# A hybrid S5, DeltaNet and expert layer on one core: decay rows by transposes, and a new deal of the z projections in the DeltaNet groups

## What is computed

```python
def chunked_gated_delta_rule(q, k, v, g, beta):
    ...
    g = jnp.cumsum(g, axis=-1)
    decay = jnp.exp(jnp.where(incl, g[..., :, None] - g[..., None, :], -jnp.inf))
    kb = k * beta[..., None]
    a_mat = jnp.where(strict, jnp.einsum('bhncd,bhnsd->bhncs', kb, k) * decay, 0.0)
    lower = a_mat + jnp.eye(C, dtype=a_mat.dtype)
    rhs = jnp.concatenate([v * beta[..., None], kb * jnp.exp(g)[..., None]], axis=-1)
    sol = lax.linalg.triangular_solve(lower, rhs, left_side=True, lower=True, unit_diagonal=True)
    ...
    attn_intra = jnp.where(incl, jnp.einsum('bhncd,bhnsd->bhncs', q, k) * decay, 0.0)
    ...

def deltanet_branch(qkv, z, beta_logit, decay_logit, conv_w, a_log, dt_bias, norm_w, w_dn_out):
    ...
    o = chunked_gated_delta_rule(q, k, v, g, beta)
    o = o * lax.rsqrt(jnp.mean(jnp.square(o), axis=-1, keepdims=True) + RMS_EPS)
    o = o * norm_w.astype(f32) * jax.nn.silu(z.astype(f32).reshape(bsz, T, DN_V_HEADS, DN_HEAD_DIM))
```

## Time and profile before

| | |
|---|---|
| median of 3 runs | 2986.1 us |
| the profiled execution | 2986.08 us, span 2984.3 us |
| busy: PE, PE's weight loads | 2900.1 us (97%), 2086.5 us (70%) |
| busy: DVE, ACT, POOL | 912.0, 517.6, 100.5 us |
| mean granted TensorE clock | 0.992 |
| DeltaNet groups | about 67 to 983 us |
| S5 and the outputs | to about 1990 us |
| experts | from there to the end |

### The profile page before, as it was taken

The page is one execution under the profiler, slowest core; times in us unless marked ns, Lnnn a source line. Parts: engine busy times, 40 slices in busy tenths (PEclk is TensorE's granted clock), DMA queues, the critical chain, the costliest instruction groups (busy, mean ns, idle before and its releaser), DMA issues.

```text
span 2984.3 us, 47457 instructions
## 1 busy us (share of the span) xinstructions
PE 2900.1 (97%) x19639; PEld 2086.5 (70%) x19639; DVE 912.0 (31%) x2066; ACT 517.6 (17%) x809; POOL 100.5 (3%) x179
## 2 busy tenths in 40 slices
PE   8999999999999999999999999999999999999996
PEld 7888788888888888888888888873444444444442
DVE  1433424424334307777730000130121112111214
ACT  2221222222212132111010000121111111112110
POOL 2010011000100000000000000000000000000000
PEclk9999999999999999999999999999999999999998
DMA  6243342332434524244347665258899999999996
GB/s 195 81 131 99 98 125 91 101 123 80 138 94 113 154 95 136 92 127 128 122 145 218 197 194 171 112 204 361 362 422 422 422 422 422 422 422 422 422 422 261
DMA packets 325775, 654.05 MB, mean 219 GB/s; under 512 B 45232, under 2 KB 274736, under 8 KB 275440
## 3 DMA queue, kind: packets, MB, share of 16 engines
q1 hardware_dynamic: 325616, 651.61, 59.4%
HBM read 649.49 MB, written 2.10 MB: 218 GB/s over the span
## 4 chain that ended last, share of the span: by engine, by line
PE 58%; issue 16%; DVE 12%; DMA 6%; DVEq 2%; ACT 1%; POOLq 1%; POOL 1%; SPq 1%; ACTq 0%
PE bank L938 11%; PE bank L632 10%; PE bank L1108 9%; PE bank L1142 7%; DMA arena<-in_w_up_dram 6%; DVE arena L1759 4%; PE bank L1086 4%; PE bank L972 4%; PE bank L1165 4%; DVE arena L1761 3%; DVE arena L1763 3%; PE bank L706 1%; PE bank L724 1%; PE bank L717 1%; PE bank L1119 1%
## 5 line engine op out<-in xcount | busy, mean ns | idle before, releaser
L632 PE MATMUL bank<-arena 128*128 128x256 f32 x4096 | 934.0, 383 | 0.0
L632 PEld LDWEIGHTS bank<-arena 128*128 128x128 f32 x4096 | 765.3, 190 | 112.6 <-issue 8.0
L1108 PE MATMUL bank<-arena 128*64 128x512 f32 x2048 | 447.0, 595 | 6.2 <-DMA arena<-in_w_up_dram 6.2
L1108 PEld LDWEIGHTS bank<-arena 128*64 128x64 f32 x2048 | 145.1, 137 | 306.1 <-issue 290.1
L938 PE MATMUL bank<-arena 128*128 128x256 f32 x1536 | 331.8, 379 | 0.0
L938 PEld LDWEIGHTS bank<-arena 128*128 128x128 f32 x1536 | 291.8, 190 | 39.9 <-issue 0.3
L1142 PE MATMUL bank<-arena 128*64 128x512 f32 x1024 | 223.3, 594 | 7.7 <-ACT masks L1466 7.7
L877 PE MATMUL bank<-arena 128*128 128x256 f32 x1024 | 223.5, 380 | 0.0
L877 PEld LDWEIGHTS bank<-arena 128*128 128x128 f32 x1024 | 194.0, 190 | 27.3 <-issue 1.0
L1142 PEld LDWEIGHTS bank<-arena 128*64 128x64 f32 x1024 | 72.1, 137 | 148.5 <-issue 137.0
L2023 DVE TENSOR_SCALAR arena<-bank 128x512 f32<-128x512 f32 x16 | 11.1, 692 | 473.7 <-PE bank L1108 473.7
(11 more groups left out here) (307 smaller groups left out, 2001.4 us busy)
## 6 DMA issues: line engine op xcount, KB each, us to landing
arena<-in_w_in_dram SPq DMA_DIRECT2D x72, 2048.0 KB, 8.7
arena<-in_w_up_dram SPq DMA_DIRECT2D x64, 2048.0 KB, 15.9
arena<-in_w_gate_dram SPq DMA_DIRECT2D x64, 2048.0 KB, 13.4
arena<-in_w_down_dram SPq DMA_DIRECT2D x64, 2048.0 KB, 20.6
arena<-in_w_dn_out_dram SPq DMA_DIRECT2D x16, 2048.0 KB, 8.5
arena<-in_w_glu_b_dram SPq DMA_DIRECT2D x8, 2048.0 KB, 8.2
arena<-in_w_glu_a_dram SPq DMA_DIRECT2D x8, 2048.0 KB, 8.3
arena<-in_w_mix_out_dram SPq DMA_DIRECT2D x8, 2048.0 KB, 13.7
```

Source lines behind the costliest of these rows:

```text
L632: last = mm(ps[bank][:, ct * T:ct * T + T], ring[:, buf, k, ct * P:ct * P + P], rhs[:, k, :], start=k == 0, stop=k == KD - 1)
L1108: last = mm(ps[bank][CAP * o:CAP * o + CAP, :], xg[:, 4 * q + k, CAP * o:CAP * o + CAP], w[:, o, k], start=False, stop=q == 3 and k == 3, ...
```

## The change

Four edits:
- POOL no longer makes `gU`; it copies the 4 columns of cumulative log decay (`gcum`) of the group. PE transposes each column, repeated 128 times by a stride of zero, in place of the product with ones: 4 transposes of 128x128 for one product of 128x512. The result is the same matrix.
- z0 is dealt out as 19 steps ahead of the first level, 2 at each of the six levels and the last one in the joining step; before it was 16, and 2 at eight places.
- z1 has one step at each of the first five levels, then 3 at the last level (before 1), 1 and 2 in the joining step, and 4, 3, 6, 4, 4 behind it (before 4, 3, 6, 4, 9).
- The first 4 steps of the next group's q projection stand ahead of L785; `front` starts at step 4. After the last group the same holds for the first slot of S5.

```diff
@@ pool
-                    g.tensor_copy(ggrp[:, c], glog[:, c, ds(GV * gi, GV)])
-                    pool.drain()
-                    for a in range(GV):
-                        g.tensor_scalar(gU[:, c, a], upper, ggrp[:, c, a:a + 1], None, ALU.mult)
+                    g.tensor_copy(ggrp[:, c], gcum[:, c, ds(GV * gi, GV)])
@@ front
-                for r in range(3):
+                part(16 * (2 * g + 1), 0, 0, 2 * g, xT, 4, 2 * KD)
+                for r in range(1, 3):
@@ decay_products
-                    mm(ps[3 + 2 * c][:, :], ones[:, :], gU[:, c].rearrange("p a t -> p (a t)"),
-                       start=True, stop=True).then_inc(gb_ready, 1)
+                    for a in range(GV):
+                        last = tr(ps[3 + 2 * c][:, a * P:a * P + P], ggrp[:, c, a:a + 1].to_broadcast([P, P]), ident[:, :])
+                    last.then_inc(gb_ready, 1)
@@ group, ahead of the levels
-                z0(0, 16)
+                z0(0, 19)
@@ in each level
-                    z0(16 + 2 * lv, 18 + 2 * lv)
+                    z0(19 + 2 * lv, 21 + 2 * lv)
...
-                    z1(lv, lv + 1)
+                    z1(lv, lv + 1 if whole else 8)
@@ joining step
-                z0(16 + 2 * lv, 18 + 2 * lv)
+                z0(31, 2 * KD)
+                z1(8, 9)
...
-                z0(16 + 2 * LEVELS, 2 * KD)
+                z1(9, 11)
@@ apply
-                z1(6, 10)
+                z1(11, 15)
...
-                z1(10, 13)
+                z1(15, 18)
...
-                z1(13, 19)
+                z1(18, 24)
...
-                z1(19, 23)
+                z1(24, 28)
...
-                z1(23, 2 * KD)
+                z1(28, 2 * KD)
+                part(16 * (2 * g + 3), 0, 0, 2 * g + 2, xT, 0, 4)
@@ after the last group
-            u_slot(0)
+            part(16 * (2 * GROUPS + 1), 0, 0, U_USE, xT, 4, 2 * KD)
```

More of the change, by code:

```diff
@@ L148, in build @@
         w0 = SH + 9984
-        gU = at(w0, 2, GV, P)
         Dc = at(w0 + 1024, 2, GV, P)
```

## The result

The changed kernel takes 2961.65 us (median of 4 runs, 2958.3 to 2965.32) beside 2984.68 us for the kernel before (now a median of 4 runs, 2981.47 to 2987.63); the ratio is 0.9925, 95% interval 0.9910 to 0.9941. That is faster by 0.75%, clear of the noise, as forecast. The forecast 2965.4 is 3.8 us above the measured time, and the range began at 2962.5, 0.85 us above it. In the two profiled executions the span goes from 2984.3 to 2961.1 us, 23.2 us where 20.7 were forecast. The profiled executions of two later variants, z0_undone and tr_twice_second, took 7438 and 6064 us, with PE at less than half its pace from start to end, so nothing is read from them and both variants were run again.

A forecast was written before the change was run, and what follows sets the result against it. PE, busy 97% of the span, was taken to bound the kernel: 0.43 + 1.30 + 0.86 = 2.59 us per group, 20.7 us over 8 groups, gave 2986.1 - 20.7 = 2965.4 us, range 2962.5 to 2970.2.

The forecast's parts named there:

- What bounds it, and that the gain arrives: Whole kernel: PE busy 97% of the span; later stages start when PE gets there, so the gain reaches the end.
- Item 1, transposes: Two places per group: four transposes at 0.109 us each replace a 0.86 us product, saving 0.43 us each.
- The upper bound: Transpose spacing of 0.188 us, from a strided row at the kernel's start; four would cost 0.75 us and save 0.11.
- the slow end of the range: Dear transposes at 0.188 us each: gain 2.18 us per group, 17.4 in all, 2968.7 us before run spread, 2970.2 with it.
- The first place: Transposes for c = 0, before the last 14 steps of the fourth projection, on PE's path: 0.43 us gained.
- the second: Second place of the transposes, in a stretch closed by a DVE chain: its 0.43 us counts only in Item 2.
- transposes without overlap: Rival: transposes take 0.27 us each, leaving 1.5 us gain per group, 12 us in all, 2974 us; chance 0.03.
- a clock that falls by them: Rival: each of 16 transpose blocks brings a clock drop of 1.77 us, 28.3 us lost, 2993.7 us; chance 0.02.
- Item 2: Ahead of the first level: three more z0 steps fill the 1.08 us wait, stretch stays 11.16 us; gain 1.30 us per group.
- Item 5 and the margins: Four q steps ahead of L785: zero gain, 1.3 us margin; without them a 0.4 us wait. Chunk 0's copy: 0.16 us margin.
- Item 3, joining step: Two more z1 steps ahead of the last step of the inverse, second set starting as before: gain 0.86 us per group.
- The sum's reference: Median of the kernel before, 2986.1 us, from which the 20.7 us gain was subtracted.

The follow-up runs named there:

- z0_undone: Changed kernel with 16 instead of 19 z0 steps ahead of the first level; 2968.8 us, and 2974.18 us when run again (_b).
- tr_twice_second: Changed kernel with the second chunk's four transposes issued twice; no total time given; when run again (_b), period 116.6 to 116.8 us over the first three groups.
- after_again: The changed kernel once more, nothing altered; 2961.08 us beside 2983.37 for the kernel before, ratio 0.9927.
- tr_only: Kernel before with only the transposes changed, steps dealt as before; 2983.2 us beside 2983.37, ratio 0.9997.
- join_undone: Changed kernel with one z1 step instead of three ahead of the joining step; 2974.0 us beside 2983.66 for the kernel before, ratio 0.9967.
- fill: Changed kernel with 20 z0 steps ahead of the first level, four z1 ahead of the joining step, six q steps ahead of L785; 2952.29 us, ratio 0.9895 to before.

## Why the prediction came out as it did

*What bounds it, and that the gain arrives*: right. PE's milestones behind the groups moved with the groups; the part behind them gave back 3.3 us in one pair of traces, 2.4 of them with a low clock at the first expert, and in after_again it gave back nothing (2001.9 us, the q steps counted in, beside 2003.4 and 2004.9 before).

*Item 1, transposes*: right, at 0.109 us each; a repeated column is read as a contiguous one. The upper bound was a misreading. The text took 0.188 us for the cost of a step of 16 elements, but that row of 32 has two paces, seen when it is asked for in parts:

```profile
8.51 4.90 PE L612 MATMUL bank<-ident,arena 128*128 128x128 f32 x22 [8.51 <-DMA arena<-in_x_dram]
...
13.70 0.84 PE L612 MATMUL bank<-ident,arena 128*128 128x128 f32 x6
```

The last of each part lasts 0.39 and 0.28 us, so the spacing is (4.90 - 0.39)/21 = 0.21 us and then (0.84 - 0.28)/5 = 0.11, with the same step of 16. The pace changes at 13.3 us (13.8 in the changed kernel), just where the trace's record of the granted clock begins, at full. A clock at its lower level up to there would fit this, though no row shows it; the stride does not fit. The forecast did not use the 0.188, but the slow end of the range did.

The first place is on the path (0.45 us by tr_only), the second is swallowed. Neither transposes without overlap nor a clock that falls by them occurred: no group of the changed kernel shows a fall, with 18 transposes in each.

*Item 2*: right, 11.16 us to the hundredth; 1.2 us by z0_undone_b for the 1.30 of the text. *Item 5 and the margins*: right, and the steps cover 0.53 us, where the text had 0.4 (the wait itself is 0.28).

*Item 3, joining step*: its 0.86 us per group is right (0.9 by join_undone), but this is the step that failed. The text priced the waits at the time that moved into them. They cost more: in 5 of 32 groups the granted clock fell behind them, for some 3.2 us. That is 0.5 us per group or 4 us per execution on average (an estimate from four profiles, with the same 4 us by the mean clocks), which the change removes as well: about 1.4 us per group at this place, where the sum had 0.86. The text looked for a clock that falls through the new transposes, in a rival and at 1.77 us a drop, and not for one that was falling already behind the old waits, at 3.2; the fifth group of the trace before, at 78.97 us beside 75.8, was there to be seen, but the text took the window of the second group for all eight.

*The sum's reference*: three runs were too few for it. The start-up in the profile was 3.3 us longer than usual, and the median of before went from 2986.1 to 2984.68 with a fourth run; three later sets gave 2983.4 (15 runs), 2983.7 (11) and 2986.2 (13). The forecast ratio, 0.9931, lies inside the measured interval. From 2984.68 the same sum gives 2964.0 and the same range begins at 2961.1, below the measured time. So that the number fell outside and not inside is in part luck. The spread of these runs does not tell how much of the missing 0.85 us is the falls and how much the reference: steady periods (20.7) and falls (4) together are more than the 23.0 and 22.3 us measured, though within their intervals.

## What to carry to other kernels

Price a short wait on a nearly full PE by an experiment that lengthens it, not by its idle time: the two pieces of work around it no longer overlap, and the clock may fall behind it. Compare all repeats of a stage before one of them stands for all: a single repeat that is 3 us longer is a cost with a chance. And where steps are dealt out by hand, aim for a few tenths of a microsecond beyond the last wait; in fill the surplus step cost nothing, since it was taken from a place with more cover.

## What the hardware showed that was not expected

- Behind waits of 0.84 and 0.80 us in the joining step the granted clock went from 1.00 to 0.5 in 5 of 8 groups; behind a single wait of 1.50 us at the first level it did so in none of 16 (z0_undone_b and tr_only). Why the one place brings it and the other doesn't was not tried.
- A wait of 0.20 us between two sets of 64x64 matmuls costs 0.42 us from start to start (1.05 against 0.63 in tr_twice_b and 0.62 in fill); without it both sets run on as one row.
- fp32 transposes of a column repeated by a stride of zero start every 0.109 us, like contiguous ones. With a step of 16 elements they started every 0.11 us too, once the pace had changed at 13.3 us, and every 0.21 before, with nothing but such transposes on PE around the change.
